# Expert weight transfers of pairs 5 to 14, issued in turn from two queues

## The reference

```python
for e in range(N_EXPERTS):                      # 32
    u = t @ w1[e] + b1[e]                       # 1024 x 2048
    glu = jnp.minimum(u[:, :D_EXPERT], SWIGLU_LIMIT)
    lin = jnp.clip(u[:, D_EXPERT:], -SWIGLU_LIMIT, SWIGLU_LIMIT)
    a = glu * jax.nn.sigmoid(SWIGLU_ALPHA * glu) * (lin + 1.0)
    out = out + gates[:, e:e + 1] * (a @ w2[e] + b2[e])     # w2: 1024 x 1024
```

## Time and profile before

| | |
|---|---|
| median of three runs | 1118.06 us |
| profiled execution | 1117.48 us |
| its span | 1115.7 us |
| busy share PE / VectorE / ScalarE | 96% / 30% / 18% |
| read from memory | 437.08 MB, 393 GB/s over the span |
| share of the chain that ended last | PE 75%, DMA 22% |

### The profile page before, as it was taken

The page is one execution under the profiler, slowest core; times in us unless marked ns, Lnnn a source line. Parts: engine busy times, 40 slices in busy tenths (PEclk is TensorE's granted clock), DMA queues, the critical chain, the costliest instruction groups (busy, mean ns, idle before and its releaser), DMA issues.

```text
span 1115.7 us, 12719 instructions
## 1 busy us (share of the span) xinstructions
PE 1070.7 (96%) x5198; PEld 505.3 (45%) x5198; DVE 334.5 (30%) x607; ACT 196.9 (18%) x338; POOL 39.5 (4%) x60
## 2 busy tenths in 40 slices
PE   8999999999999999999999898989898989898998
PEld 8888888734344343434343333333242424232432
DVE  4888767323122121212212121112121212021212
ACT  7676684500000000100000000000000000000000
POOL 1225020000000000000000000000000000000000
PEclk9999999999999999999999999999999999999999
DMA  9764349999999999999999999999999999999997
GB/s 361 297 206 138 125 166 426 392 419 428 429 426 428 427 428 428 432 431 432 432 431 432 431 432 432 432 432 432 432 431 430 432 432 431 431 432 431 425 426 287
DMA packets 27844, 438.66 MB, mean 393 GB/s; under 512 B 3232, under 2 KB 3488, under 8 KB 6560
## 3 DMA queue, kind: packets, MB, share of 16 engines
q1 hardware_dynamic: 26928, 431.46, 91.8%
q10 hardware_dynamic: 880, 6.69, 1.4%
HBM read 437.08 MB, written 1.05 MB: 393 GB/s over the span
## 4 chain that ended last, share of the span: by engine, by line
PE 75%; DMA 22%; ACT 1%; DVE 1%; issue 0%; SPq 0%; ACTq 0%
PE bank L957 23%; DMA ring<-in_expert_q 22%; PE bank L983 20%; PE bank L526 12%; PE bank L925 6%; PE bank L888 5%; PE bank L513 3%; PE bank L807 2%; PE bank L577 2%; DMA ring<-in_head_w 1%; PE bank L626 0%; PE bank L923 0%; PE bank L653 0%; PE bank L652 0%; PE bank L614 0%
## 5 line engine op out<-in xcount | busy, mean ns | idle before, releaser
L957 PE MATMUL bank<-ring,feat_r 128*64 128x512 f32 x1504 | 334.1, 597 | 13.1 <-DMA ring<-in_expert_q 13.1
L957 PEld LDWEIGHTS bank<-ring,feat_r 128*64 128x64 f32 x1504 | 104.5, 137 | 232.7 <-issue 209.4
L983 PE MATMUL bank<-ring,feat_r 128*64 128x512 f32 x768 | 173.1, 596 | 12.3 <-DMA ring<-in_expert_q 11.8
L1755 DVE TENSOR_SCALAR late_r<-bank 128x512 f32<-128x512 f32 x32 | 22.1, 692 | 422.2 <-PE bank L957 422.2
L526 PE MATMUL bank<-ring_s,feat_s 128*128 128x512 f32 (+2 forms) x428 | 129.7, 384 | 0.6 <-DVE ring_s L1420 0.5
L957 PE MATMUL bank<-pool_r,feat_r 128*64 128x512 f32 x512 | 118.3, 609 | 10.6 <-DMA pool_r<-in_expert_q 10.5
L983 PEld LDWEIGHTS bank<-ring,feat_r 128*64 128x64 f32 x768 | 54.0, 137 | 118.0 <-issue 114.4
L1364 ACT ACTIVATE late_r<-late_r 128x512 f32<-128x512 f32 x32 | 20.2, 630 | 469.1 <-DVE late_r L1755 469.1
L1779 DVE TENSOR_TENSOR acc_r<-bank,acc_r 128x512 f32<-128x512 f32 x64 | 44.3, 691 | 151.0 <-PE bank L925 151.0
L526 PEld LDWEIGHTS bank<-ring_s,feat_s 128*128 128x128 f32 x428 | 76.5, 188 | 13.8 <-issue 1.8
L526 PE MATMUL bank<-ring_s 128*128 128x512 f32 (+2 forms) x212 | 79.7, 376 | 0.0
(11 more groups left out here) (216 smaller groups left out, 672.5 us busy)
## 6 DMA issues: line engine op xcount, KB each, us to landing
ring<-in_expert_q SPq DMA_DIRECT2D x45, 4096.0 KB, 27.4
ring<-in_expert_q SPq DMA_DIRECT2D x41, 2048.0 KB, 19.5
pool_r<-in_expert_q SPq DMA_DIRECT2D x15, 4096.0 KB, 29.1
pool_r<-in_expert_q SPq DMA_DIRECT2D x16, 2048.0 KB, 20.1
ring<-in_head_w SPq DMA_DIRECT2D x23, 1024.0 KB, 5.0
ring<-in_expert_q SPq DMA_DIRECT2D x21, 1024.0 KB, 16.0
ring<-in_head_w SPq DMA_DIRECT2D x6, 768.0 KB, 10.6
qkT_r<-in_expert_q ACTq DMA_DIRECT2D x1, 2048.0 KB, 14.0
```

What stands on the lines that cost most here:

```text
L957: mm = pe.matmul(b[e * SLOTS:(e + 1) * SLOTS, :], xT[:, k, e * SLOTS:(e + 1) * SLOTS], w[:, e, g, :], start=(late and k == 0), stop=(k == ...
L983: mm = pe.matmul(bank[4 + h][e * SLOTS:(e + 1) * SLOTS, :], aT[k // 4][:, k % 4, e * SLOTS:(e + 1) * SLOTS], w[:, q, e, :], start=(k == 0) ...
L1755: ts(glu, bank[2 * f][:], LIMIT, None, ALU.min).then_inc(sem(f"glu_ready{f}"), 1)
```

## The change

In the loop over pairs 5 to 14 SyncE issues only the even quads, 0, 2 and 4, of each pair. ScalarE issues the odd ones: quad 5 of a pair behind its sigmoid of f = 0, quad 1 of the next pair behind its sigmoid of f = 1, and quad 3 of the next pair behind the pair's last copy. The waits before each issue are those of before. ScalarE's loop takes two pairs in one turn. Pairs 0 to 4 and the last pair are loaded as before.

```diff
+        def load_quad(eng, i, q, pair, cycle):
+
+            at = i * JOB_CHUNKS // 2 + q
+            eng.wait_ge(ring_used, CYCLE * cycle + NHEAD + FRONT + 2 * at + 1 - WIDE + 1)
+            eng.dma_start(quad(at), expert_q[pair, q]).then_inc(landed[quad_slot(at)], 16)
...
             with sp.Fori(0, LAST) as j:
                 for i in range(2):
-                    load_pair(i, FRONT_PAIRS + 2 * j + i, j)
+                    for q in range(0, JOB_CHUNKS // 2, 2):
+                        load_quad(sp, i, q, FRONT_PAIRS + 2 * j + i, j)
...
-            def pair(j, first=False, second=False):
+            def pair(j, first=False, second=False, loads=(None, None)):
                 for f in range(2):
                     act.wait_ge(sem(f"glu_ready{f}"), j + 1)
                     act.activation(sig, glu, ACT.Sigmoid, scale=ALPHA).then_inc(sem(f"sig_ready{f}"), 1)
+                    if loads[f] is not None:
+                        load_quad(act, *loads[f])
                     act.wait_ge(sem(f"act_turned{f}"), j + 1)
...
-            pair(FRONT_PAIRS - 1, second=True)
-            with act.Fori(FRONT_PAIRS, PAIRS) as j:
-                pair(j)
+            pair(FRONT_PAIRS - 1, second=True, loads=(None, (0, 1, FRONT_PAIRS, 0)))
+            load_quad(act, 0, 3, FRONT_PAIRS, 0)
+
+            def two_pairs(j, more):
+
+                p_ = FRONT_PAIRS + 2 * j
+                pair(p_, loads=((0, 5, p_, j), (1, 1, p_ + 1, j)))
+                load_quad(act, 1, 3, p_ + 1, j)
+                pair(p_ + 1, loads=((1, 5, p_ + 1, j), (0, 1, p_ + 2, j + 1) if more else None))
+                if more:
+                    load_quad(act, 0, 3, p_ + 2, j + 1)
+
+            with act.Fori(0, LAST - 1) as j:
+                two_pairs(j, True)
+            two_pairs(LAST - 1, False)
+            pair(PAIRS - 1)
```

More of the change, by code:

```diff
@@ L366, in load_pair @@
             def load_pair(i, pair, cycle):
[L368 to L371, removed]
+                for q in range(JOB_CHUNKS // 2):
+                    load_quad(sp, i, q, pair, cycle)
             with sp.Fori(0, LAST) as j:
                 for i in range(2):
-                    load_pair(i, FRONT_PAIRS + 2 * j + i, j)
+                    for q in range(0, JOB_CHUNKS // 2, 2):
+                        load_quad(sp, i, q, FRONT_PAIRS + 2 * j + i, j)
             def end_home(c):
```

## The result

Six runs of the changed kernel took 1122.97 to 1126.63 us, median 1124.39, against 1117.73 for the kernel before: a ratio of 1.0063 (95% interval 1.0053 to 1.0074), slower by 6.7 us. Five more on another chip gave a median of 1123.16, ratio 1.0053 [1.0040, 1.0066]. The forecast was 1123.4, with a range of 1117.3 to 1126.4.

What follows compares the result with a forecast made beforehand. Transfers were taken to bound pairs 5 to 14, with PE work alone at the end. Order 6.5, rate -1.3 and clock +0.6 sum to +5.8 us; 1117.5 + 5.8 = 1123.3, stated as 1123.4, range 1117.3 to 1126.4.

Steps and rivals of the forecast that it cites:

- What bounds the kernel: Pairs 5 to 14 run at the pace of the transfers; behind quad 4 of pair 14 come 73.3 us of PE work.
- Issue instructions and their place: Thirty quad issues moved to ScalarE's queue, standing some 1.5 us later behind a sigmoid: cost 0 on the path.
- Order of transfer: Two filled queues share about equally, so even quads land late and the end with them: 6.5 us, ends 3.9 and 9.7.
- settled distance f: Time from an even quad's landing (SyncE) to the next odd one's (ScalarE): about 5 to 6 us, then staying.
- Quad 3: Odd quads 2.5 to 3 us late; PE's wait before quad 3 gone or small, about 5 us before quad 4.
- Rate: Up to quad 4 of pair 14, a second filled queue hides transfers' fixed part: -1.3 us, ends 0 and -6.5.
- rival that pays the loss back: Second queue hides all 0.11 us fixed per transfer, -6.5 against +6.5: about 1118.5 us; chance 0.13.
- Clock: TensorE's clock may fall behind the last quad wait: 0 to 1.7 us, taken as 0.6.
- Strict order between queues: Queues serve strictly in order of issue, with 1.3 us gained: 1116.5 us; part of a group with chance 0.12.
- late issues on ScalarE: An issue on ScalarE holds up the copy for PE in each pair; same time as the forecast; chance 0.03.
- faster: Queues settle half a turn apart and hidden fixed part exceeds the delay: 1115.2 us; chance 0.12 together with strict order.
- larger delay: f near 0 and a clock fall at the end: +11.4 us, 1128.9 us; chance 0.05.

## Why the prediction was right

*What bounds the kernel.* Right, and the step that decided: PE's waits keep their sum in a pair (4.9 us), and the loss is that of one landing, carried on by 73.3 us of PE's work.

*Issue instructions and their place.* Right at 0: 77 issues on ScalarE gave 0.9996.

*Order of transfer.* The mechanism is shown by the quad moved alone (landings within 0.2 us of what equal shares give) and by giving quads back. The term was 6.5 and measured 5.6. The settled distance f was wrong: I reckoned 5 to 6. Quads 2 and 3 of pair 14 in the changed kernel, by their issues:

```profile
L299 SPq DMA_DIRECT2D ring<-in_expert_q x1: 333/333/333, 997.8 to 997.8; - x1
...
DMA to landing us min/median/max: 26.9/26.9/26.9
...
L299 ACTq DMA_DIRECT2D ring<-in_expert_q x1: 335/335/335, 1006.6 to 1006.6; - x1
...
DMA to landing us min/median/max: 27.4/27.4/27.4
```

They land at 1024.7 and 1034.0, so f is 9.3. At quads 2 and 3 of pair 5, where 5 to 6 was reckoned, it came out at 7.3, and it did not stay: 9.2 at the next two and 9.3 from pair 6 on. Nor does the program alone fix it. Four more profiles have the same schedule over pairs 6 to 10; the distance settled at 9.3 once more in the changed kernel, at 8.3 in the kernel with pair 14 given back, at 7.9 in the one with the hand-over at pair 11 and at 10.8 in the one with the last quad given back. The formula 9.71 - f/2 holds roughly. Quad 4 of pair 13 was late by 5.6, 6.8 and 4.4 us where f was 9.3, 8.3 and 10.8, and the formula gives 5.1, 5.6 and 4.3. My reckoning took the 16 DMA engines as one. The landing is that of the last of them, and their semaphore increments for the first quad of pair 5 stand 4.1 us apart in the kernel before and 7.4 in the changed one. That this moved f and makes up the rest of the formula is argued, not shown.

*Quad 3.* I held that the odd quads would be early enough. At f = 9.3 they are late by about as much as the even ones, so the predicted pattern, one wait of 5 us before quad 4, did not appear: the waits were 0.3, 2.2 and 2.4 where they had been 0.3, 2.6 and 2.0. Giving back the last quad showed that quad 3 alone can hold the end late by 3.3 us.

*Rate.* Taken as -1.3, measured 0: 431 GB/s against 432. The Trainium skill's rule ("DMA: Bandwidth & Descriptors", section "Rules for kernel authors") that spreading over queues brings no bandwidth is what the trace shows here. The rival that pays the loss back falls with it.

*Clock.* Taken as 0.6. In the profiled execution it did not fall behind the last wait (granted 1.00 from 1044 us on), so 0 there: 5.6 + 0 + 0 against 5.5 measured. The median of six is 6.7 above; the further 1.2 us have no shown cause. Two candidates stand in the rows: a fall of the clock behind the last wait, worth up to 1.7 us, and another f, for at 8.3 the even quads were 1.2 us later than at 9.3.

*The sum.* That 5.8 came so near to the 5.5 of the profiled execution is luck: the order of transfer was 0.9 too large, the rate 1.3 too low and the clock 0.6 too large, and these errors cancel to 0.2. Within the order term the wrong f made 1.4 too much and the formula 0.5 too little. The sign, the share that the queues take and the place where it is felt are not luck. (One rival's time is off on paper: strict order with 1.3 us gained gives 1117.5 - 1.3 = 1116.2, not 1116.5. Nothing hangs on it.)

*Strict order between queues* and *late issues on ScalarE*, two of the rivals, are excluded by the quad moved alone and by the kernel with all 77 issues on ScalarE. The *faster* case needed f from 10 on together with a hidden fixed part: f of 10.8 did occur, in the kernel with the last quad given back, but no gain in rate did. The *larger delay* needed f near 0 behind pair 5; no profile has it.

## What to carry to other kernels

Where a stream of transfers bounds the kernel and is used in order, a second filled queue did not speed it up (431 against 432 GB/s). It let a later transfer take half of the rate from an earlier one, and a single transfer on an empty queue made the one before it late by a whole transfer's time, 9.9 us. What this costs is read at the end: the lateness of each landing less its room. PE catches it up if waits enough follow (18 of 60 quads moved early cost nothing). It does not if the hand-over lies near the end, or is so rough that the queues run dry (5 us). Moving all issues of the ordered stream to another engine was free when the whole stream went.

## What the runs showed of the hardware

Two filled issuing queues shared the DMA engines about equally at transfers of 4 MB: the quad moved alone landed at 1042.2 us and made quad 4 late by 9.9 us, both within 0.2 us of what equal shares give. Together they carried 431 GB/s, and one alone 432. The distance from a landing on SyncE's queue to the next on ScalarE's settled at values from 7.9 to 10.8 us in five profiled executions with the same schedule, and stayed within 0.1 us from pair 8 on. Transfers over 64 of the 128 partitions reached 211 GB/s on one queue and 260 on two, with the DMA share at 1.00 in both: a busy share of 1.00 does not mean that the engines carry what they can.

The length of a wait alone did not decide whether the clock fell. Two waits of 2.2 us in the changed kernel:

```profile
626.00 5.35 PE L962 MATMUL bank<-pool_r,feat_r 128*64 128x512 f32 x16 [2.17 <-DMA pool_r<-in_expert_q]
...
917.49 3.65 PE L962 MATMUL bank<-ring,feat_r 128*64 128x512 f32 x16 [2.22 <-DMA ring<-in_expert_q]
```

Behind the first the granted clock fell to 0.50 (626.5 to 629.9 us), that is 1.2 GHz, and 16 products took 5.35 us; behind the second it was 1.00, or 2.4 GHz, and they took 3.65. In the kernel before it fell behind three waits of 2.6 us (at 621, 679 and 737 us) and stayed in full behind five later ones of the same length.
